# Three edits around the layer norms: how the deviation is found, who splits the first gate tile, and where three side products land

## The chip, the cores and the metric

The kernel runs on one core of a Trainium2 chip. A core has a matrix engine (TensorE, in rows PE, with its weight loads as PEld), a vector engine (VectorE, DVE), a scalar engine with function tables (ScalarE, ACT), GpSimd (POOL) and a sync engine that issues DMAs (SP). They run side by side and wait for each other by semaphores. The metric is the device time of one execution in microseconds. Times inside a profile are microseconds from the start of its span; unless said otherwise, they are of the first of the two layers.

## The reference

The input x has 512 tokens of width 2048. Two layers follow each other. Each makes y from x (the first by an attention of three branches and a gated recurrence, the second by a gated causal convolution of 31 taps with a layer norm of its own, then a product with an output matrix), and then both do the same, which is where the change lies:

```
mu  = mean(x);  var = mean((x - mu)**2)
layernorm(x) = (x - mu) * rsqrt(var + 1e-5) * g + b
x = layernorm(1.414 * x + y)                       # post norm of the layer
x = x + (p[i] @ ple_w[i]) * sigmoid(x @ ple_gate_w[i])
```

p[i] has 512 tokens of width 256, ple_w[i] is 256 x 2048 (the side product), ple_gate_w[i] is 2048 x 2048 (the gate). Everything is float32. There are three layer norms in all: the post norms of the two layers (numbers 0 and 2 in the code) and the one inside the convolution layer (number 1).

## The kernel before

Activations lie transposed: 16 chunks of 128 channels by 512 tokens, in SBUF buffers Y and Z. A weight matrix is a row of tiles of 128 x 2048 (all 16 input chunks for 128 output channels), 177 in all, counted by W_... constants. To keep float32 accuracy on fast matmuls, every operand is taken as a high and a low part: ACT rounds a tile into w_hi (`split` in the scalar block, line 769), then DVE (line 1117), or GpSimd in the convolution (line 363), forms w_lo as w_raw - w_hi. A gemm of one output chunk is 16 x 3 matmuls of 128 x 512: high by high, high by low, low by high (line 419 is the helper that issues all matmuls). SP loads the tiles into two slots; a tile's load waits until the tile that last had its slot is split, by the semaphore w_split, which counts splits in the order of the tiles. Gemms put their result into two PSUM banks G0 and G1 in turns; G_... constants count these uses, and bank_free0 and bank_free1 count how often each was emptied. Six more banks, X0 to X2 and T0 to T2, serve everything else. Each engine's order is written out by hand in its own block.

The stretch of the change is `second_part`, which stands in the blocks of PE, ACT and DVE and is run once per layer, with its counterpart `x1_low` on GpSimd:

1. The output projection: 16 gemms. DVE adds each result to the residual, subtracts a shift (the mean over the first channels), and adds up the values (ln_sum) and, from ACT's squares, the squares (ln_sqs). The last of these additions are lines 1456, 1462 and 1465; both inputs of each lie in SBUF.
2. The PLE pack: eight side products of this half of ple_w (c = 0 to 7), six matmuls each, which ACT copies from G0 or G1 into Z (`ple_out`, line 934). Between them PE does the norm's small work, in this order: products 0 and 1; `token_mean` and `token_var`, eight matmuls of one column each, that bring ln_sum into X0 and ln_sqs into T2, by token; products 2 and 3; `spread_mean` (two matmuls, a diagonal matrix by ones, into X1); product 4; `spread_dev` (the same for 1/deviation, into X2); products 5, 6 and 7.
3. `statistics` on DVE: mean, offset and variance as columns of four (lines 1477 to 1484), the mean's diagonal (line 1472), the split of the first gate tile, three small steps of Newton's method that refine ACT's guess of 1/deviation (lines 1491 to 1496), and its diagonal. The guess is made by `deviation` on ACT: logarithm, then exponential of minus half of it (lines 958 and 960). The two functions lie in different tables, each loaded ahead of it.
4. The chunks, j = 0 to 15: DVE subtracts the mean in X1 (line 1501, three ahead) and multiplies by 1/deviation in X2 (line 1505). ACT applies g and b (line 997), then rounds the chunk into a_hi (`x1_high`, line 773). GpSimd makes a_lo (line 340). ACT also empties side products 5 to 7 behind chunks 0, 1 and 2, and splits the second gate tile behind chunk 6; DVE forms its low part behind chunk 9.
5. The gate: `gemm_pair` runs the first two gate gemms interleaved, the second six chunks behind the first, and takes each chunk when its low part is there. Then 14 gemms follow. DVE combines, and GpSimd stores.

The layer norm of the convolution uses the same `statistics` and `deviation`; between its spread of the mean and that of the deviation PE does a whole gemm.

## Time and profile before

| | us |
|---|---|
| median of three timed runs | 2190.28 |
| the three runs | 2190.28, 2190.56, 2186.19 |
| the profiled execution | 2185.88 |
| its span (first to last instruction) | 2184.1 |
| mean granted TensorE clock, as a share of full | 0.994 |
| TensorE matmuls busy | 2148.8 (98%) |
| DVE busy | 1220.6 (56%) |
| ACT busy | 801.1 (37%) |
| GpSimd busy | 341.8 (16%) |

The busy shares are averages over very different stages. TensorE's matmuls overlap each other, so its 98% says that it seldom stands still, not that it runs at its peak. The profile also names, for each idle time, what ended it, and follows the chain of work that ended last back from the end: 95% of it are on PE.

### The profile page before, as it was taken

The page shows a single profiled execution, that of the slowest core. Times are in us where ns is not written, and L with a number is a line of the kernel's source. Part 1 is how long each engine was busy: PE and PEld are TensorE (multiplying, and loading weights), DVE is VectorE, ACT ScalarE, POOL GpSimd, SP SyncE. Part 2 cuts the span into 40 slices and gives each one's busy share as a digit, 9 for nine tenths or more (in the row PEclk, how much of TensorE's full clock was granted, in tenths as well). Part 3 has the DMA queues.
Part 4 walks back from the last instruction along what each step waited for, and adds up shares of the span by engine and source line. Part 5 has one row for each costly group of instructions (what it writes and reads, how often), then busy time and mean ns, then how long its engine had stood idle before and what let it go on. Part 6 is the DMA issues. An engine that isn't in the chain of part 4 may idle for free.

```text
span 2184.1 us, 27326 instructions
## 1 busy us (share of the span) xinstructions
PE 2148.8 (98%) x9916; PEld 1764.0 (81%) x9916; DVE 1220.6 (56%) x1986; ACT 801.1 (37%) x990; POOL 341.8 (16%) x179
## 2 busy tenths in 40 slices
PE   8999999999999999999899999999999999999998
PEld 7888878888888888788688778888888788886887
DVE  5224464554645646436733388888888764466332
ACT  3224364453544645312622232222323442126221
POOL 0000000000000000000300024444757430003000
PEclk9999999999999999999999999999999999999999
DMA  8222221122122212422233322222222234221331
GB/s 317 80 97 77 78 78 69 66 77 77 58 77 77 77 64 77 148 96 96 78 120 120 120 93 96 97 97 96 96 96 97 94 115 155 96 96 58 127 121 60
DMA packets 31551, 213.77 MB, mean 98 GB/s; under 512 B 3744, under 2 KB 3744, under 8 KB 7296
## 3 DMA queue, kind: packets, MB, share of 16 engines
q1 hardware_dynamic: 26928, 189.80, 24.3%
q0 software_dynamic: 4560, 23.20, 2.7%
q8 instruction: 31, 0.51, 0.1%
q14 instruction: 32, 0.26, 0.0%
HBM read 204.60 MB, written 8.39 MB: 98 GB/s over the span
## 4 chain that ended last, share of the span: by engine, by line
PE 95%; ACT 2%; DVE 1%; issue 1%; DMA 0%; POOL 0%; SPq 0%; DVEq 0%; ACTq 0%; POOLq 0%
PE G L419 86%; PE X L419 7%; PE T L419 1%; PE T L558 1%; ACT w_hi L769 1%; ACT Y L997 1%; DMA Z<-xT_in 0%; DVE w_lo L1117 0%; ACT a_hi L773 0%; DVE a_lo L1122 0%; POOL a_lo L340 0%; PE T L663 0%; DVE tmp L1472 0%; ACT Z L934 0%; DVE Y L1501 0%
## 5 line engine op out<-in xcount | busy, mean ns | idle before, releaser
L419 PE MATMUL G<-a_hi,w_hi 128*128 128x512 f32 (+1 forms) x2784 | 1092.4, 393 | 21.3 <-POOL a_lo L340 10.9
L419 PE MATMUL G<-a_lo,w_hi 128*128 128x512 f32 (+1 forms) x2784 | 1081.5, 389 | 0.0
L419 PE MATMUL G<-a_hi,w_lo 128*128 128x512 f32 x2752 | 1074.0, 390 | 0.0
L769 ACT ACTIVATE w_hi<-w_raw 128x2048 fp32r<-128x2048 f32 x175 | 335.1, 1915 | 1107.4 <-PE G L419 1103.1
L1117 DVE TENSOR_TENSOR w_lo<-w_raw,w_hi 128x2048 fp32r<-128x2048 f32 x128 | 293.5, 2293 | 691.8 <-ACT w_hi L769 691.8
L419 PEld LDWEIGHTS G<-a_hi,w_hi 128*128 128x128 f32 x2784 | 524.6, 188 | 138.9 <-POOL a_lo L340 16.2
L419 PEld LDWEIGHTS G<-a_lo,w_hi 128*128 128x128 f32 x2784 | 524.8, 189 | 107.7 <-issue 1.5
L419 PEld LDWEIGHTS G<-a_hi,w_lo 128*128 128x128 f32 x2752 | 518.2, 188 | 109.1
L1638 DVE SCALAR_TENSOR_TENSOR T<-tmp,par,T 128x512 f32<-128x512 f32 x464 | 306.9, 748 | 0.0
L363 POOL TENSOR_TENSOR w_lo<-w_raw,w_hi 128x2048 fp32r<-128x2048 f32 x46 | 212.5, 4619 | 247.8 <-ACT w_hi L769 247.8
L334 POOL DMA_DIRECT2D Y<-xT_in x4 | 2.1, 532 | 848.0 <-DVE a_lo L1122 848.0
L340 POOL TENSOR_TENSOR a_lo<-Y,a_hi 128x512 fp32r<-128x512 f32 x32 | 42.1, 1342 | 361.9 <-ACT a_hi L773 361.9
L419 PE MATMUL X<-Z 128*128 128x64 f32 (+7 forms) x544 | 96.5, 325 | 0.0
L419 PEld LDWEIGHTS X<-Z 128*128 128x128 f32 (+2 forms) x544 | 72.5, 181 | 22.9 <-issue 13.3
L1328 DVE COPY_PREDICATED tmp<-msk,X 128x256 f32<-128x256 uint8 (+2 forms) x48 | 23.4, 487 | 52.3 <-issue 34.8
L773 ACT ACTIVATE a_hi<-Y 128x512 fp32r<-128x512 f32 x80 | 47.0, 622 | 10.2 <-PE G L419 8.4
L1626 DVE TENSOR_TENSOR tmp<-G,tmp 128x512 f32<-128x512 f32 x16 | 11.0, 687 | 58.0 <-PE G L419 58.0
L952 ACT ACTIVATE tmp<-Y 128x512 f32 (+1 forms) x32 | 19.5, 630 | 63.9 <-DVE Y L1539 58.2
L847 ACT ACTIVATE Z<-Z,nmx 128x128 f32<-128x128 f32 (+1 forms) x64 | 35.2, 552 | 17.1 <-DVE nmx L1360 17.0
L1122 DVE TENSOR_TENSOR a_lo<-Y,a_hi 128x512 fp32r<-128x512 f32 x48 | 30.7, 686 | 14.5 <-ACT a_hi L773 14.4
L1501 DVE TENSOR_TENSOR Y<-Y,X 128x512 f32<-128x512 f32 x48 | 32.2, 678 | 11.6 <-PE X L419 11.6
L952 ACT ACTIVATE Z<-Y 128x512 f32 (+1 forms) x16 | 10.1, 633 | 77.6 <-POOL Y L380 72.8
(234 smaller groups left out, 1438.0 us busy)
## 6 DMA issues: line engine op xcount, KB each, us to landing
w_raw<-wall_in SPq DMA_DIRECT2D x175, 1024.0 KB, 4.8
Z<-xT_in SPq DMA_DIRECT2D x4, 1024.0 KB, 11.3
Y<-w_in POOLq DMA_DIRECT2D x2, 2048.0 KB, 18.9
Y<-xT_in POOLq DMA_DIRECT2D x4, 1024.0 KB, 5.0
x_residual<-Y POOLq DMA_DIRECT2D x16, 256.0 KB, 3.8
Y<-x_residual POOLq DMA_DIRECT2D x4, 1024.0 KB, 5.8
out<-Y POOLq DMA_DIRECT2D x16, 256.0 KB, 3.6
w_raw<-wall_in SPq DMA_DIRECT2D x8, 256.0 KB, 10.3
```

The lines of the kernel that those rows point to most:

```text
L340: pool.tensor_tensor(a_lo[:, j, :], chunk(Y, j), a_hi[:, j, :].bitcast(F), ALU.subtract).then_inc(S(f"x1_split{layer}"), 1)
L363: pool.tensor_tensor(w_lo[:, w.slot, :], w_raw[:, w.slot, :], w_hi[:, w.slot, :].bitcast(F), ALU.subtract).then_inc(S("w_split"), 1)
L419: return pe.matmul(o, l, r, start=start, stop=stop)
L769: f(w_hi[:, w.slot, :], w_raw[:, w.slot, :], ACT.Copy).then_inc(S("w_hi"), 1)
L773: f(a_hi[:, j, :], chunk(Y, j), ACT.Copy).then_inc(S(sem), 1)
L847: f(prob_of(ti), prob_of(ti), ACT.Exp, bias=nmx[:, o + ti:o + ti + 1], accum_out=rsum[:, o + ti:o + ti + 1]).then_inc(S("exps"), 1)
L952: f(dst, chunk(Y, c), ACT.Square).then_inc(S("squared"), 1)
L1117: tt(w_lo[:, w.slot, :], w_raw[:, w.slot, :], w_hi[:, w.slot, :].bitcast(F), ALU.subtract).then_inc(S("w_split"), 1)
L1122: tt(a_lo[:, j, :], src, a_hi[:, j, :].bitcast(F), ALU.subtract).then_inc(S(sem), 1)
L1328: dve.copy_predicated(dst[0:rows], m[0:rows], src[0:rows]).then_inc(S("level_copied"), 1)
L1501: tt(chunk(Y, j), chunk(Y, j), X[1][:, :], ALU.subtract).then_inc(S("less_mean"), 1)
L1638: stt(acc, src, cw, acc, op0=ALU.mult, op1=ALU.add).then_inc(S("tap"), 1)
```

## The change

`deviation` on ACT is now one square root. DVE takes its reciprocal as the guess, and no longer splits the first gate tile between the mean's diagonal and the Newton steps. A square root into a scratch column, `load_root_table`, stands earlier in ACT's order, so that the table is loaded there: ahead of the split of the first gate tile in `second_part`, and behind `silu_z(40, 8)` in the convolution. The first gate tile's low part is made by GpSimd, at the head of `x1_low`. Side products 5 to 7 of the second pack of each layer go into the banks T0, T1 and X0 and wait for none of them; the G counts shift by three per layer. ACT copies them behind the sixteenth chunk. DVE waits for the first gate tile's split before it splits the second, behind chunk 9.

```diff
--- before.py
+++ after.py
@@ -53,10 +53,11 @@
 W_CONV = 95
 W_TILES = 177
 
-G_PLE = ((61, 85), (157, 181))
-G_OUT = (69, 165)
-G_GATE = (93, 189)
-G_CONV = 109
+G_PLE = ((61, 85), (154, 178))
+G_OUT = (69, 162)
+G_GATE = (90, 183)
+G_CONV = 106
+LATE = 5
 LEVEL_ROWS = (64, 96, 128, 128, 128, 128)
 
 HALVES = (64, 32, 16, 8, 4, 2, 1)
@@ -109,7 +110,7 @@
 
 LN_COUNTS = dict(
     half_summed=4, shift_done=1, shift_ready=1, sums_set=3, centred=16, c_summed=16, squared=16, sq_summed=16, mean_sum=1,
-    var_sum=1, ln_step=6, var=1, ln_log=1, ln_guess=1, diag_d=1, diag_r=1, mean_spread=1, dev_spread=1, less_mean=16, normed=16)
+    var_sum=1, ln_step=6, var=1, ln_root=1, ln_guess=1, diag_d=1, diag_r=1, mean_spread=1, dev_spread=1, less_mean=16, normed=16)
 
 
 class Idx:
@@ -184,6 +185,7 @@
         rsum = sb("rsum", [P, 12])
         rg = sb("rg", [P, 12])
         eglast = sb("eglast", [P, NT])
+        act_scratch = sb("act_scratch", [P, 1])[:, :]
         stat = sb("stat", [P, 5 * NT])
         lb = sb("lb", [P, 4, HEADS])
         ident = par[:, C_ID:C_ID + P]
@@ -259,6 +261,7 @@
         X = [pb("X0"), pb("X1"), pb("X2")]
         TB = [pb("T0"), pb("T1"), pb("T2")]
         O = X[0]
+        LATE_BANKS = (TB[0], TB[1], X[0])
         NEAR_BANKS = (X[1], TB[2])
         LEVEL_AT = (None, (X[2], 0), (X[2], 256), (X[0], 0), (X[0], 256), (X[1], 0), (X[1], 256))
         LEVEL_BANK_DONE = (1, 3, 3, 5, 5, 7, 7)
@@ -335,6 +338,11 @@
 
             def x1_low(layer):
 
+                w = Idx(W_GATE[layer])
+                pool.wait_ge(S("w_hi"), w.n(1))
+                pool.wait_ge(S("w_split"), w.n())
+                pool.tensor_tensor(w_lo[:, w.slot, :], w_raw[:, w.slot, :], w_hi[:, w.slot, :].bitcast(F),
+                                   ALU.subtract).then_inc(S("w_split"), 1)
                 for j in range(KC):
                     pool.wait_ge(S(f"x1_hi{layer}"), j + 1)
                     pool.tensor_tensor(a_lo[:, j, :], chunk(Y, j), a_hi[:, j, :].bitcast(F), ALU.subtract).then_inc(
@@ -479,9 +487,12 @@
                     if c == 0:
                         pe.wait_ge(S("w_split"), w.n(1))
                         pe.wait_ge(S("p_split"), layer + 1)
-                    g = Idx(G_PLE[layer][u] + c)
-                    pe.wait_ge(S(f"bank_free{g.slot}"), g.half())
-                    o = G[g.slot][:, :]
+                    if u == 1 and c >= LATE:
+                        o = LATE_BANKS[c - LATE][:, :]
+                    else:
+                        g = Idx(G_PLE[layer][u] + c)
+                        pe.wait_ge(S(f"bank_free{g.slot}"), g.half())
+                        o = G[g.slot][:, :]
                     for k in range(PLE_K):
                         at = (c * PLE_K + k) * P
                         hi, lo = w_hi[:, w.slot, at:at + P], w_lo[:, w.slot, at:at + P]
@@ -931,7 +942,10 @@
                     act.wait_ge(S("gemm_done"), W_PLE[layer][u] + 1)
                 else:
                     act.wait_ge(S("ple_done"), 14 * layer + 7 * u + c + 1)
-                frees(f(chunk(Z, 8 * u + c), G[g.slot][:, :], ACT.Copy), g)
+                if u == 1 and c >= LATE:
+                    f(chunk(Z, 8 * u + c), LATE_BANKS[c - LATE][:, :], ACT.Copy)
+                else:
+                    frees(f(chunk(Z, 8 * u + c), G[g.slot][:, :], ACT.Copy), g)
 
 
             prev_hz(HEADS, Idx(W_PLE[0][0] - 1))
@@ -955,9 +969,10 @@
 
                 var, dev = stat[:, 2 * NT:3 * NT], stat[:, 3 * NT:4 * NT]
                 act.wait_ge(*after("var", n, 1))
-                f(dev, var, ACT.Ln).then_inc(S("ln_log"), 1)
-                act.wait_ge(*after("ln_log", n, 1))
-                f(dev, dev, ACT.Exp, scale=-0.5).then_inc(S("ln_guess"), 1)
+                f(dev, var, ACT.Sqrt).then_inc(S("ln_root"), 1)
+
+            def load_root_table():
+                f(act_scratch, ones[:, 0:1], ACT.Sqrt)
 
             def second_part(layer):
                 w, g = W_OUT[layer], G_OUT[layer]
@@ -980,6 +995,7 @@
                             c = 3 + 2 * k + n
                             square(n_ln, i * 4 + c, ln_sq[c % 2], i * 4 + (c - 1))
 
+                load_root_table()
                 split(Idx(w + 17))
                 square(n_ln, KC - 1, ln_sq[1], KC - 2)
                 ple_out(layer, 1, 0)
@@ -1000,10 +1016,11 @@
                         x1_high(j - 1)
                     elif j < 3:
                         x1_high(j)
-                        ple_out(layer, 1, j + 5)
                     if j == 6:
                         split(Idx(w + 18))
                 x1_high(KC - 1)
+                for c in range(LATE, 8):
+                    ple_out(layer, 1, c)
 
                 def gate(w, g, n_out):
                     act.wait_ge(S("gemm_done"), w.n(1))
@@ -1078,6 +1095,7 @@
 
             split(Idx(W_CONV + 42))
             silu_z(40, 8)
+            load_root_table()
             square(1, KC - 2, c_sq[0], KC - 2)
             square(1, KC - 1, c_sq[1], None)
             deviation(1)
@@ -1464,7 +1482,7 @@
                 dve.wait_ge(*after("sq_summed", n, c))
                 tt(sqs, sqs, sq, ALU.add).then_inc(S("sq_summed"), 1)
 
-            def statistics(n, diag_of_mean, between=None):
+            def statistics(n, diag_of_mean):
 
                 mean, off, var, dev, rr = [stat[:, k * NT:(k + 1) * NT] for k in range(5)]
 
@@ -1484,9 +1502,8 @@
                 stt(var, TB[2][:, 0:NT], 1.0 / D, off, op0=ALU.mult, op1=ALU.add).then_inc(S("var"), 1)
                 dve.wait_ge(*after("centred", n, KC))
                 spread(diag_of_mean, mean).then_inc(S("diag_d"), 1)
-                if between:
-                    between()
-
+                dve.wait_ge(*after("ln_root", n, 1))
+                dve.reciprocal(dev, dev).then_inc(S("ln_guess"), 1)
                 dve.wait_ge(*after("ln_guess", n, 1))
                 stt(rr, dev, -0.5, dev, op0=ALU.mult, op1=ALU.mult).then_inc(step, 1)
                 dve.wait_ge(*after("ln_step", n, 4))
@@ -1568,7 +1585,7 @@
                 dve.wait_ge(*drained(Idx(g + 15)))
                 centre(n_ln, KC - 1)
                 add_last(n_ln, KC - 1, ln_sqs, ln_sq[1])
-                statistics(n_ln, diag_d, lambda: split(Idx(w + 17)))
+                statistics(n_ln, diag_d)
                 dve.wait_ge(*after("mean_spread", n_ln, 1))
                 for j in range(3):
                     minus_mean(j)
@@ -1578,6 +1595,7 @@
                     if j + 3 < KC:
                         minus_mean(j + 3)
                     if j == 9:
+                        dve.wait_ge(S("w_split"), w + 18)
                         split(Idx(w + 18))
 
                 def gate(g, j, n_gate):
```

## Rows read from the trace of the kernel before

**Rows 1.** The page, part 1: engine, busy us (share of the span), instructions.
```profile
PE 2148.8 (98%) x9916; PEld 1764.0 (81%) x9916; DVE 1220.6 (56%) x1986; ACT 801.1 (37%) x990; POOL 341.8 (16%) x179
```
**Rows 2.** The view of waits, TensorE: in total, times, longest.
```profile
PE G L419 <- POOL a_lo L340: 10.9, 10, 2.9
```
**Rows 3.** The chain that ended last: start us, us, engine, tile and line.
```profile
1067.95 0.49 ACT Z L934
...
1076.53 1.81 ACT w_hi L769
...
1079.63 2.17 POOL a_lo L340
...
1733.02 0.86 PE X L419 x2
```
**Rows 4.** Timeline of ACT: start, us, engine, line, operation [idle before, releaser].
```profile
1055.37 1.92 ACT L769 ACTIVATE w_hi<-w_raw 128x2048 fp32r<-128x2048 f32 x1 [3.90 <-PE G L419]
1057.20 0.61 ACT L952 ACTIVATE tmp<-Y 128x512 f32<-128x512 f32 x1
...
1058.79 1.28 ACT L958 ACT_TABLE_LOAD   x1
1060.09 0.20 ACT L958 ACTIVATE stat<-stat 128x4 f32<-128x4 f32 x1
...
1096.50 1.92 ACT L769 ACTIVATE w_hi<-w_raw 128x2048 fp32r<-128x2048 f32 x1 [6.61 <-PE G L419]
```
**Rows 5.** Timeline of DVE, in the same columns.
```profile
1056.76 0.69 DVE L1462 TENSOR_TENSOR tmp<-tmp,Y 128x512 f32<-128x512 f32 x1
1057.84 0.69 DVE L1465 TENSOR_TENSOR tmp<-tmp 128x512 f32<-128x512 f32 x1 [0.39 <-ACT tmp L952]
...
1059.83 0.16 DVE L1484 SCALAR_TENSOR_TENSOR stat<-T,stat 128x4 f32<-128x4 f32 x1 [0.40 <-PE T L419]
...
1063.90 1.87 DVE L1501 TENSOR_TENSOR Y<-Y,X 128x512 f32<-128x512 f32 x3
1065.75 0.69 DVE L1505 TENSOR_TENSOR Y<-Y,X 128x512 f32<-128x512 f32 x1
...
1077.11 0.68 DVE L1501 TENSOR_TENSOR Y<-Y,X 128x512 f32<-128x512 f32 x1
1078.36 2.29 DVE L1117 TENSOR_TENSOR w_lo<-w_raw,w_hi 128x2048 fp32r<-128x2048 f32 x1 [0.57 <-ACT w_hi L769]
...
1733.91 0.69 DVE L1501 TENSOR_TENSOR Y<-Y,X 128x512 f32<-128x512 f32 x1 [11.55 <-PE X L419]
```
**Rows 6.** Timeline of TensorE: the variance matmuls and the two spreads.
```profile
1058.69 1.03 PE L419 MATMUL T<-ones,tmp 128*128 128x1 f32 x8
...
1062.44 1.02 PE L419 MATMUL X<-tmp,ones 128*128 128x512 f32 x2
...
1064.68 1.02 PE L419 MATMUL X<-tmp,ones 128*128 128x512 f32 x2
```
**Rows 7.** Lines 1456 and 340 (min/median/max ns), and timelines of DVE and GpSimd.
```profile
L1456 DVE TENSOR_TENSOR Y<-Y,tmp x4: 678/692/3907, 1056.0 to 1977.9; 128x512 f32<-128x512 f32 x4
...
L340 POOL TENSOR_TENSOR a_lo<-Y,a_hi x32: 1276/1289/2158, 1068.0 to 2013.6; 128x512 fp32r<-128x512 f32 x32
...
1779.53 4.60 POOL L363 TENSOR_TENSOR w_lo<-w_raw,w_hi 128x2048 fp32r<-128x2048 f32 x1 [6.25 <-ACT w_hi L769]
1780.04 4.64 DVE L1663 TENSOR_TENSOR Y<-Y,Z 128x512 f32<-128x512 f32 x1 [5.61 <-ACT Z L1051]
```
**Rows 8.** Timeline of TensorE behind the convolution norm and at the second layer's gate.
```profile
1719.35 1.91 PE L419 MATMUL X<-tmp,ones 128*128 128x512 f32 x2 [0.93 <-DVE tmp L1472]
...
1723.10 0.40 PE L419 MATMUL G<-a_hi,w_lo 128*128 128x512 f32 x1
...
2003.72 0.80 PE L419 MATMUL G<-a_hi,w_hi 128*128 128x512 f32 x1 [2.22 <-POOL a_lo L340]
...
2010.02 0.40 PE L419 MATMUL G<-a_hi,w_hi 128*128 128x512 f32 x1
```

## The prediction

> **What bounds the kernel now.** I read the page first. TensorE is busy for 98% of the span [rows 1], so an edit pays only where TensorE waits. The view of waits names the largest wait: its matmuls wait for GpSimd's low parts, 10.9 us in ten places [rows 2]. The chain of waits puts them: after the output projection of each of the two layers, where the post norm runs. Among its links there are ACT's side-product copies, its weight split, and one GpSimd row of 2.17 us, behind which the gate matmuls go on at 1081.84 [rows 3]. Then I read this stretch engine by engine [rows 4, 5, 6]. The second layer repeats it 921.9 us later with the same distances to a few hundredths, so I work out the first and double it.
>
> The profiled execution took 2185.88 us, of which 1.78 lie outside its span of 2184.1. The median of the three timed runs is 2190.28; one of them is at 2186.19. The sum is made on the profiled one.
>
> **Root and reciprocal.** Two table loads go (each as the one from 1058.79 to 1060.09, 1.30 us [rows 4]), and so does a DVE split inside the statistics, of 2.29 us like that of 1078.36 [rows 5]. One load comes ahead of the weight split at 1055.37; ACT is idle for 3.90 us before that [rows 4], so it is hidden. But what do the norms wait for? The deviations are spread by a TensorE pair at 1064.68, which stands in program order behind side products 2 to 4 and the mean's pair at 1062.44 [rows 6]. Without loads and split the diagonal is done about 1062.0: variance at 1059.83 + 0.16 = 1059.99, root and reciprocal about 0.2 each like the four-column rows, three steps of 0.2, one of 0.7. So 2.7 us of slack hide it. What a root and a reciprocal of four columns take, no row here shows: between nothing and the 0.69 of a 512-column DVE row, both inside the slack. What is late next is TensorE itself. The mean's pair lands at 1062.44 + 0.89 = 1063.33, where DVE began at 1063.90 [rows 5]; the deviations' pair at 1064.68 + 0.89 = 1065.57, where DVE began at 1065.75. (0.89 is what lies between such a pair's start at 1733.02 and its reader's at 1733.91 [rows 3, 5].) Gain: 0.18 us per layer. In the convolution's norm nothing waits for the deviations until a whole gemm later: 0.
>
> By the Trainium skill, page "ScalarE: Activation LUTs", section "What ACT_TABLE_LOAD costs", each switch takes about 2.66 us with its drain; the rows have 1.30 from the load's start to the activation's. By the page two loads would be worth 5.3 us on ACT, by the rows 2.6; in the sum both are 0.18.
>
> **Three side products in free banks.** TensorE no longer waits for a bank at the last product and at the gate's start, some tenths; but it then waits for low parts, so that is worth 0. ACT has three copies fewer between the first chunks: 0.49 each on the chain [rows 3], 1.47 in all. GpSimd's seventh low part, asked for at 1079.63, is asked for at 1079.63 - 1.47 - 0.18 = 1077.98. It does not start then. Before, it took 2.17 us, as against a usual 1.29 [rows 7], because DVE's split of 1078.36 held it until 1080.65; it ended 1.14 behind that. Now the split starts at DVE's next slot, 1077.11 + 0.60 - 0.18 = 1077.53 (its high part is there at 1076.53 + 1.81 - 1.65 = 1076.69), ends at 1079.82, and the low part at 1080.96. The gate matmuls go on at 1081.01: gain 0.83 us per layer instead of 1.65, the 0.18 included. The three copies come back behind the last chunk, where ACT idles for 6.61 us ahead of 1096.50 [rows 4]; without that cover they would cost 1.5.
>
> **The gate's first low part on GpSimd.** Its high part is there at 1055.37 + 1.92 = 1057.29. GpSimd has no other work then: the residual's four DMA issues ahead of it in its queue were done before the first out chunk, and the low parts behind it wait for normed chunks, the first of which DVE begins at 1065.75. So it starts at about 1057.37, and takes 4.6 us. SP's next weight load waits for this split; even at 1062.1 it is issued earlier than before, and it is for ACT's row of 1096.50: 0.
>
> What runs beside it on DVE? The sum of squares, with two inputs in SBUF, at 1057.84 [rows 5]; TensorE's variance matmuls wait for it and start at 1058.69 [rows 6]. The trace shows such pairs. A DVE add of two SBUF tiles takes 0.69, and 3.91 where a GpSimd split is under way [rows 7]; one that came 0.51 us behind GpSimd's start (1780.04 behind 1779.53) took 4.64 and ended 0.55 behind GpSimd's end. DVE rows that read PSUM keep their 0.68. Here GpSimd is 0.47 ahead; DVE's sum of 1056.76 may hold it until 1057.45. Then GpSimd ends at 1062.05, the sum of squares at 1062.60 instead of 1058.53, and the variance matmuls start at 1062.65 instead of 1058.69: 3.96 us lost, with TensorE idle and all that follows in program order shifted whole (side products 2 to 7, both spreads, the norm, the low parts). The 2.7 us of slack above do not help, since variance and side products shift together. Bounds: below, 0 (no hold; nothing in it makes TensorE earlier than 1058.69, where the mean's matmuls end); above, the whole 4.6.
>
> The Trainium skill, page "SBUF — State Buffer", section "Who interferes with whom", says that a VectorE instruction with two SBUF inputs and a GpSimd one that reads SBUF exclude each other for the whole instruction, the first one winning. The rows agree (3.91 and 4.64 for 0.69). It goes further than they do: an instruction of four columns would be held too, which in the first rival below would make the loss 1.9 us per layer instead of 1.4.
>
> **The clock.** TensorE's idle 4 us stand between 16 one-column matmuls [rows 6]. In the convolution's norm 16 such matmuls and 0.93 us of idle are followed by a fall to the low level: from 1719.35 to the sixth gate matmul at 1723.10 are 3.75 us, where full clock (0.45 + 0.64 + 4 x 0.23) makes 2.01 [rows 8]: price 1.7. At the gate of the second layer 15 intervals from 2003.72 to 2010.02 take 6.30, where full clock (0.34 + 14 x 0.23) makes 3.56: price 2.7 [rows 8]. So a fall behind the new stall costs 0 to 2.7 per layer; I take 1.7, the nearest row. The fall at the gate itself stays; the idle before it is 3.9 us instead of 2.9, and its price I leave; since the two falls shown differ by 1.0, it may move by that.
>
> **Sum.** Per layer 3.96 - 0.83 + 1.7 = 4.8; two layers 9.7 us slower. On the profiled execution 2195.5, on the median 2200.0. Since the timed runs lie at both levels, I take 2198. This case's own range: 2 x 3.13 = 6.3 without falls to 2 x (3.13 + 2.7) = 11.7, that is 2192 to 2202.
>
> **Rivals.**
> 1. DVE first (0.12). If DVE's sum of squares gets in before GpSimd, GpSimd holds from 1058.53 to 1063.15, and the mean's diagonal, DVE's next 512-column row with two SBUF inputs, due at 1059.9, ends at 1063.15 + 0.65 = 1063.8, for a pair due at 1062.44: 1.4 lost, 0.8 won, 1.1 us slower in all: 2187 to 2191.4. For it: only 0.47 us separate the two. Against it: 0.51 was enough for GpSimd, and a start like its others (0.08 behind the high part) is 0.39 ahead at the least.
> 2. No hold at this place (0.10): the sum of squares keeps 0.69, since GpSimd takes the read side only after its start, more than 0.47 later. The change then wins 0.83 per layer: 1.7 faster, 2188.6; if the later low part isn't held either, it ends at 1079.3, and 2.5 per layer make 2185.3. It decides at once: any hold over 0.83 us turns it to slower. Against it: the pairs shown were held for the rest of the other engine's instruction.
> 3. The clock falls far longer than any row shows (0.06): over 2204.
> 4. The root's table isn't the one in force when it comes, and a load of 1.3 stands before it: hidden by the 2.7 us, the same time as the forecast, so no chance of its own.
>
> **How the numbers follow.** The forecast has 0.72. Range 2191 to 2203: it takes in the forecast's bounds, the upper end of rival 1, and leaves out rival 2 and the long fall. A change under 0.2% (4.4 us) can't be told from none here. Slower by more than that: the forecast but for a rest (0.70) and rival 3: 0.76. Within it: rival 1, the smaller form of rival 2, and the rest: 0.19. Faster: 0.05.
>
> **What would show it.** The sum of squares (line 1465 before) at about 4.7 us instead of 0.69 in both layers, with a GpSimd split of 4.6 from 1057.4; TensorE's variance matmuls at 1062.6 behind a wait of 4 us for DVE; a granted clock under 1 in the stretch behind. The norms then stand 3.8 us later throughout, the split of the next tile on DVE beside a GpSimd low part of 3.0 us, and the gate goes on near 1085 (1086.7 with the fall). No table load between the variance and the gates. The prediction is wrong if the sum of squares keeps 0.69, or if DVE gets in first.

## The result, and the profile after

| | before | after |
|---|---|---|
| median of five runs, us | 2187.50 | 2199.52 |
| lowest to highest | 2186.19 to 2190.56 | 2199.23 to 2201.00 |
| profiled execution | 2185.88 | 2199.23 |
| its span | 2184.1 | 2197.2 |
| mean granted TensorE clock | 0.994 | 0.992 |

The ratio is 1.0053, with an interval of 1.0038 to 1.0067: the change costs 12 us. 2198 was forecast, in a range of 2191 to 2203. The ratios, here and below, are estimates with a 95% interval and can differ in the fourth place from the quotient of the two medians. Two executions far outside all others, one of before with 9306.75 us and one of f_again with 7727.82, fell in a slow state and are left out of the medians.

The page after, part 1, in the columns of [rows 1]:

```profile
PE 2152.5 (98%) x9916; PEld 1768.2 (80%) x9916; DVE 1224.5 (56%) x1987; ACT 797.6 (36%) x987; POOL 352.3 (16%) x181
```

The busy shares hardly move, since 13 us are 0.6% of the span. The view of waits does say where they are; it is of TensorE, and answers to [rows 2]:

```profile
PE G L427 <- POOL a_lo L348: 11.7, 12, 3.7
...
PE T L427 <- DVE tmp L1483: 7.3, 2, 3.7
```

The first line is the old wait for low parts, 0.8 longer. The second is new: T is the bank of the variance, and its matmuls wait twice, 3.7 us each, for DVE's sum of squares. GpSimd and DVE in this stretch, in the columns of [rows 5], first layer:

```profile
1058.77 4.51 POOL L344 TENSOR_TENSOR w_lo<-w_raw,w_hi 128x2048 fp32r<-128x2048 f32 x1 [165.19 <-ACT w_hi L780]
...
1086.06 10.45 POOL L348 TENSOR_TENSOR a_lo<-Y,a_hi 128x512 fp32r<-128x512 f32 x7 [1.70 <-ACT a_hi L784]
```

```profile
1059.23 4.59 DVE L1483 TENSOR_TENSOR tmp<-tmp 128x512 f32<-128x512 f32 x1 [0.39 <-ACT tmp L966]
...
1066.54 0.17 DVE L1506 RECIPROCAL stat<-stat 128x4 f32<-128x4 f32 x1
...
1071.38 1.88 DVE L1518 TENSOR_TENSOR Y<-Y,X 128x512 f32<-128x512 f32 x3 [3.36 <-PE X L427]
1073.62 0.69 DVE L1522 TENSOR_TENSOR Y<-Y,X 128x512 f32<-128x512 f32 x1 [0.36 <-PE X L427]
...
1085.58 2.28 DVE L1135 TENSOR_TENSOR w_lo<-w_raw,w_hi 128x2048 fp32r<-128x2048 f32 x1
```

The sum of squares comes 0.46 us behind GpSimd's split and takes 4.59 instead of 0.69 [rows 5]. TensorE waits for it and then runs slower, as the timeline of TensorE shows:

```profile
1059.27 0.95 PE L427 MATMUL X<-ones,tmp 128*128 128x1 f32 x8
1063.88 1.87 PE L427 MATMUL T<-ones,tmp 128*128 128x1 f32 x8 [3.66 <-DVE tmp L1483]
...
1066.61 0.63 PE L427 MATMUL G<-p_hi,w_lo 128*128 128x512 f32 x1
...
1070.31 1.02 PE L427 MATMUL X<-tmp,ones 128*128 128x512 f32 x2
...
1072.56 1.02 PE L427 MATMUL X<-tmp,ones 128*128 128x512 f32 x2
...
1089.05 0.50 PE L427 MATMUL G<-a_hi,w_hi 128*128 128x512 f32 x1 [3.67 <-POOL a_lo L348]
```

The view by windows (stretch; length; busy us and instructions of PE, PEld, DVE, ACT, POOL; granted clock; DMA share; GB/s) has the granted clock at 0.50 for the five us that begin 0.88 before the end of the stall, which is the lower of its two levels (1.2 and 2.4 GHz), and at 0.84 for the next five:

```profile
1063.00:1068.00 5.00, 4.12 (x14) 3.64 (x15) 3.23 (x11) 0.21 (x1) 0.28 (x1) 0.50 0.59 210
1068.00:1073.00 5.00, 5.00 (x18) 3.50 (x17) 1.64 (x4) 1.43 (x3) 0.00 (x0) 0.84 0.00 0
```

ACT's table load is where the diff put it, under an idle time. Behind the variance there is one root and no load:

```profile
1052.88 1.28 ACT L975 ACT_TABLE_LOAD   x1
1056.77 1.92 ACT L780 ACTIVATE w_hi<-w_raw 128x2048 fp32r<-128x2048 f32 x1 [2.39 <-PE G L427]
...
1066.05 0.21 ACT L972 ACTIVATE stat<-stat 128x4 f32<-128x4 f32 x1 [5.88 <-DVE stat L1502]
```

Runs of different kernels are best laid over each other at the start of the mean's matmuls, which comes before the first thing that the change can delay. The table has, from there, where TensorE starts the variance's matmuls, the two spreads, the gate's seventh chunk (at which it takes up again after its wait), and the last matmul of the gate's pair. f_again is f_behind_diag once more, on another chip. Distances in us, read from each kernel's timeline of TensorE, first layer; in brackets the second layer.

| kernel | variance | mean's spread | deviations' spread | 7th chunk | end of pair |
|---|---|---|---|---|---|
| before | 0.81 | 4.56 | 6.80 | 23.96 (23.96) | 42.89 (44.36) |
| after | 4.61 | 11.04 | 13.29 | 29.78 (29.25) | 49.00 (48.42) |
| a_pool_only | 4.61 | 10.65 | 12.90 | 30.13 (30.20) | 49.23 (49.40) |
| b_no_pool | 0.82 | 4.56 | 6.81 | 23.47 (23.46) | 42.64 (43.87) |
| c_root_only | 0.81 | 4.56 | 6.80 | 24.10 (24.10) | 43.29 (43.08) |
| d_late_only | 0.81 | 4.56 | 6.81 | 23.30 (23.31) | 42.50 (42.22) |
| e_behind_squares | 0.82 | 6.39 | 8.74 | 25.23 (25.23) | 45.18 (44.46) |
| f_behind_diag | 0.81 | 4.56 | 6.81 | 23.30 (23.30) | 42.51 (42.50) |
| f_again | 0.81 | 4.56 | 6.80 | 23.30 (23.31) | 42.26 (42.45) |
| g_quarters | 1.37 | 6.71 | 8.96 | 25.45 (25.46) | 45.28 (44.64) |
| h_psum_square | 0.81 | 5.14 | 7.50 | 23.99 (23.99) | 44.43 (44.43) |
| i_second_split_at_8 | 0.81 | 4.56 | 6.80 | 22.58 (22.59) | 41.76 (41.80) |
| j_both_splits_early | 0.81 | 4.56 | 6.80 | 23.13 (23.12) | 40.98 (41.03) |
| k_lag_5 | 0.81 | 4.56 | 6.81 | 23.12 (23.11) | 40.74 (42.11) |

After the change the seventh chunk is 5.82 and 5.29 us later, the pair's end 6.11 and 4.06: 10.2 of the profiled span's 13.1. Of the rest, 1.4 had come before the mean's matmuls of the first layer (1059.27 against 1057.88), from clock falls at the start-up; 1.6 lie behind the first layer, where after a wait of 2.16 for a weight split the clock fell at 1270.79 and before it did not. No edit touches either place.

### The profile page after: what moved, and what is told of

Read it like the earlier page. It is cut to its first block, busy times and chain, and to the rows that moved or that the text cites. A ratio compares the mean times of both kernels' runs of the same rounds, so it can differ in the third digit from the quotient of the medians.

```text
span 2197.2 us, 27322 instructions
## 1 busy us (share of the span) xinstructions
PE 2152.5 (98%) x9916; PEld 1768.2 (80%) x9916; DVE 1224.5 (56%) x1987; ACT 797.6 (36%) x987; POOL 352.3 (16%) x181
## 4 chain that ended last, share of the span: by engine, by line
PE 95%; ACT 2%; DVE 1%; issue 1%; DMA 0%; POOL 0%; SPq 0%; DVEq 0%; ACTq 0%; POOLq 0%
PE G L427 86%; PE X L427 7%; PE T L427 1%; PE T L569 1%; ACT w_hi L780 1%; ACT Y L1013 1%; DMA Z<-xT_in 0%; DVE tmp L1483 0%; ACT a_hi L784 0%; DVE w_lo L1135 0%; DVE a_lo L1140 0%; POOL a_lo L348 0%; PE T L674 0%; PE T L679 0%; PE T L546 0%
## 5 line engine op out<-in xcount | busy, mean ns | idle before, releaser
L1135 DVE TENSOR_TENSOR w_lo<-w_raw,w_hi 128x2048 fp32r<-128x2048 f32 x126 | 288.9, 2293 | 692.4 <-ACT w_hi L780 692.4
L371 POOL TENSOR_TENSOR w_lo<-w_raw,w_hi 128x2048 fp32r<-128x2048 f32 x46 | 212.4, 4618 | 249.6 <-ACT w_hi L780 249.6
L344 POOL TENSOR_TENSOR w_lo<-w_raw,w_hi 128x2048 fp32r<-128x2048 f32 x2 | 9.0, 4508 | 332.6 <-ACT w_hi L780 332.6
L784 ACT ACTIVATE a_hi<-Y 128x512 fp32r<-128x512 f32 x80 | 46.8, 621 | 10.2 <-PE G L427 8.4
## 6 DMA issues: line engine op xcount, KB each, us to landing
Z<-xT_in SPq DMA_DIRECT2D x4, 1024.0 KB, 11.5
```

The source lines that it names most:

```text
L371: pool.tensor_tensor(w_lo[:, w.slot, :], w_raw[:, w.slot, :], w_hi[:, w.slot, :].bitcast(F), ALU.subtract).then_inc(S("w_split"), 1)
L784: f(a_hi[:, j, :], chunk(Y, j), ACT.Copy).then_inc(S(sem), 1)
L1135: tt(w_lo[:, w.slot, :], w_raw[:, w.slot, :], w_hi[:, w.slot, :].bitcast(F), ALU.subtract).then_inc(S("w_split"), 1)
```

## The experiments

The theory: the whole loss is GpSimd's split holding DVE's sum of squares, together with the clock that falls behind the stall. The rivals: the root and the late copies have a share in it; or the split costs at any place.

**a_pool_only, b_no_pool, c_root_only, d_late_only** take the change apart. From before, a_pool_only has only the split moved:

```diff
+                pool.tensor_tensor(w_lo[:, w.slot, :], w_raw[:, w.slot, :], w_hi[:, w.slot, :].bitcast(F),
+                                   ALU.subtract).then_inc(S("w_split"), 1)
...
-                statistics(n_ln, diag_d, lambda: split(Idx(w + 17)))
+                statistics(n_ln, diag_d)
```

DVE also waits for the first gate tile's split ahead of that of the second, as in the whole change. b_no_pool is the whole change with these lines turned round, c_root_only has the root and the reciprocal alone (DVE's split stays between the mean's diagonal and the reciprocal), d_late_only the three late side products alone.

> The kernel before with one edit of the three: the first gate tile's low part by GpSimd. Theory 1 (GpSimd's split holds DVE's sum of squares, and TensorE stands behind it): the whole loss is here. The sum of squares takes 4.6 us in both layers, TensorE's variance matmuls wait 3.7 us for it, the clock falls behind it. Per layer 3.8 for the hold and 1.7 to 2.7 for the fall, nothing back: 11 to 13 us slower than before, more than the full change by the 1.3 us that the side products give back. Theory 2 (the loss comes of the late side products or of the table load ahead of the weight split, and the held sum would be hidden): within 3 us of before.

> The full change without this one edit: DVE splits the first gate tile inside the statistics, as before. Theory 1: the sum of squares is back at 0.69 us, no wait of TensorE ahead of the variance matmuls, no fall of the clock there, and the late side products bring the seventh low part 0.66 us earlier per layer: 1 to 2 us faster than before (2185 to 2187 where before has 2187.5). Theory 2: still 8 us or more slower than before.

> The kernel before with one edit: root and reciprocal in place of logarithm and exponential, the table loaded ahead. The spread of the deviations is bound by TensorE's order (side products 2 to 4 ahead of it), not by ACT or DVE. Theory 1: no change, within 0.5 us in the trace from the norm to the gate. Rival: the two table loads of 1.3 us were on the way to the norm, and 2.6 us per layer come back: 5 us faster.

> The kernel before with one edit: side products 5 to 7 in T0, T1 and X0, copied behind the chunks. Theory 1 (GpSimd's seventh low part is held by DVE's split of the second gate tile): the seventh chunk's high part comes 1.47 us earlier, the low part ends only 0.6 to 0.7 earlier and takes 2.9 us instead of 2.17; gain 0.65 per layer, 1.3 us in all. Rival (the low part simply follows its chunk): it takes 1.3 us, the gate goes on 1.5 us or more earlier, 3 us faster in all.

| kernel | runs | median us | ratio to before | interval |
|---|---|---|---|---|
| a_pool_only | 5 | 2198.25 | 1.0050 | 1.0036 to 1.0064 |
| b_no_pool | 11 | 2185.40 | 0.9992 | 0.9983 to 1.0001 |
| c_root_only | 11 | 2188.53 | 1.0004 | 0.9995 to 1.0013 |
| d_late_only | 11 | 2185.01 | 0.9986 | 0.9977 to 0.9995 |

The median of before on that chip was 2186.74. The split alone costs 11.5, where the whole change costs 12, and without it nothing is lost. It had been expected to cost 1.3 more than the whole change, which has the late side products' gain. The traces bear that out, with a seventh chunk 0.35 and 0.95 later than after's in the two layers; the medians, from two chips, do not, and their intervals are too wide to tell. Its rows on DVE and TensorE are those of after:

```profile
1059.36 4.60 DVE L1470 TENSOR_TENSOR tmp<-tmp 128x512 f32<-128x512 f32 x1 [0.39 <-ACT tmp L957]
```

```profile
1064.01 1.87 PE L424 MATMUL T<-ones,tmp 128*128 128x1 f32 x8 [3.66 <-DVE tmp L1470]
```

d_late_only brings the seventh chunk forward by 0.66 per layer. c_root_only brings nothing: in the table its spreads stand where they stood, and the seventh chunk is 0.14 later. DVE's timeline has the reason:

```profile
1062.73 2.28 DVE L1121 TENSOR_TENSOR w_lo<-w_raw,w_hi 128x2048 fp32r<-128x2048 f32 x1
1064.93 0.17 DVE L1494 RECIPROCAL stat<-stat 128x4 f32<-128x4 f32 x1
...
1066.33 1.88 DVE L1506 TENSOR_TENSOR Y<-Y,X 128x512 f32<-128x512 f32 x3
1068.13 0.68 DVE L1510 TENSOR_TENSOR Y<-Y,X 128x512 f32<-128x512 f32 x1
```

With the split still on DVE, its rows from the mean's diagonal to the norm follow each other without idle time, and the reciprocal's 0.20 adds to them. Counted from the mean's matmuls (1060.10), the subtractions begin at 6.23 instead of 6.02 and the first product with 1/deviation at 8.03 instead of 7.87. b_no_pool has both rows too, and its seventh chunk is 0.17 behind d_late_only's. With the split on GpSimd and out of the way DVE waits for the spreads, and the reciprocal costs nothing: f_behind_diag, below, has 23.30 like d_late_only.

**e_behind_squares, f_behind_diag**: where does the split cost nothing? Both are the whole change, with GpSimd made to wait ahead of its split, for the last sum of squares or for the deviations' diagonal:

```diff
+                pool.wait_ge(*after("sq_summed", 2 * layer, KC))    # e_behind_squares
+                pool.wait_ge(*after("diag_r", 2 * layer, 1))        # f_behind_diag
                 pool.wait_ge(S("w_hi"), w.n(1))
```

> The full change, but GpSimd's split of the first gate tile waits until DVE's sum of squares is done, and so comes between that and the mean's diagonal. Theory 1, form A (every DVE instruction with two SBUF inputs is held, four columns too): the sum of squares keeps 0.69, and the offset step (four columns, both inputs the mean) waits for the end of GpSimd's 4.5 us; the mean's diagonal comes 1.9 us late for TensorE; 1.9 - 0.66 per layer, 2.5 us slower than before in all, more if the clock falls. Form B (only the wide instructions are held): the offset step takes 0.16, the diagonal of 512 columns waits: 1.2 to 1.3 late, 1.2 us slower in all. Theory 2 (no hold by GpSimd): no wait at all, 1.3 us faster than before.

> The full change, but GpSimd's split waits until DVE has made the deviations' diagonal. From there on DVE's instructions read PSUM on one side. Theory 1: no DVE instruction is held; the split lies beside the subtractions of the mean and is over before the first low part; TensorE's stalls are those of the kernel with DVE's split in its old place: 1 to 2 us faster than before. Rival (a GpSimd split beside these subtractions slows them too, or comes too late for the gate): subtractions over 0.7 us, or a wait of the first gate matmul, and no gain.

The median of before on this chip was 2186.56, for these two and the next two. e_behind_squares: 2191.30 (7 runs), ratio 1.0022 (1.0011 to 1.0034). f_behind_diag: 2184.91 (11 runs), ratio 0.9994 (0.9985 to 1.0003). The timeline of DVE in e_behind_squares:

```profile
1057.61 0.69 DVE L1484 TENSOR_TENSOR tmp<-tmp 128x512 f32<-128x512 f32 x1 [0.39 <-ACT tmp L967]
1058.64 0.16 DVE L1496 TENSOR_SCALAR stat<-X 128x4 f32<-128x4 f32 x1 [0.34 <-PE X L428]
1058.84 4.14 DVE L1498 SCALAR_TENSOR_TENSOR stat<-stat 128x4 f32<-128x4 f32 x1
```

and its split on GpSimd:

```profile
1058.39 4.58 POOL L345 TENSOR_TENSOR w_lo<-w_raw,w_hi 128x2048 fp32r<-128x2048 f32 x1 [166.44 <-DVE tmp L1484]
```

The sum of squares is free again at 0.69. The mean's columns, read from a PSUM bank, keep 0.16 inside the split. The next row is four columns wide, has both inputs in SBUF, and takes 4.14, to 1062.98, where the split ends at 1062.97. So an instruction of four columns is held like one of 512, which [rows 7] did not show. The seventh chunk is 1.27 later per layer than before, which makes the 2.5 expected; the pair's end is 2.3 later in the first layer and 0.1 in the second, and the median 4.7. What makes up the difference is not shown; I take it for the spread of clock falls, and can't put it to one row. There is no fall behind this stall itself, though TensorE waits 1.66 us for the mean's diagonal:

```profile
1064.04 1.13 PE L428 MATMUL X<-tmp,ones 128*128 128x512 f32 x2 [1.66 <-DVE tmp L1491]
...
1065.23 0.40 PE L428 MATMUL G<-p_lo,w_hi 128*128 128x512 f32 x1
```

The matmuls behind it keep 0.40, and the granted clock from 1064 to 1069 is 1.00.

In f_behind_diag the split stands beside rows that read the spreads in PSUM. Both engines keep their times:

```profile
1061.81 4.58 POOL L345 TENSOR_TENSOR w_lo<-w_raw,w_hi 128x2048 fp32r<-128x2048 f32 x1 [169.92 <-DVE tmp L1491]
...
1077.92 5.43 POOL L349 TENSOR_TENSOR a_lo<-Y,a_hi 128x512 fp32r<-128x512 f32 x3 [1.70 <-ACT a_hi L785]
```

```profile
1063.23 1.88 DVE L1519 TENSOR_TENSOR Y<-Y,X 128x512 f32<-128x512 f32 x3 [1.50 <-PE X L428]
1065.48 0.69 DVE L1523 TENSOR_TENSOR Y<-Y,X 128x512 f32<-128x512 f32 x1 [0.37 <-PE X L428]
...
1077.44 2.28 DVE L1136 TENSOR_TENSOR w_lo<-w_raw,w_hi 128x2048 fp32r<-128x2048 f32 x1
```

The last row is the bound that is left: DVE's split of the second gate tile at 1077.44 stands 0.48 ahead of GpSimd's seventh low part, the first of the three at 1077.92, which takes 2.94, not 1.29. TensorE goes on when it has ended, at 1080.91.

**g_quarters, h_psum_square**: what exactly is held? g_quarters makes GpSimd's split four instructions of 512 columns. h_psum_square takes away one of the two SBUF inputs of the sum of squares, by having ACT square the last chunk into bank T0:

```diff
+                for q in range(4):                                   # g_quarters
+                    last = pool.tensor_tensor(w_lo[:, w.slot, quarter(q)], w_raw[:, w.slot, quarter(q)], ...
...
-                square(n_ln, KC - 1, ln_sq[1], KC - 2)               # h_psum_square
+                square(n_ln, KC - 1, TB[0][:, :], None)
...
-                add_last(n_ln, KC - 1, ln_sqs, ln_sq[1])
+                add_last(n_ln, KC - 1, ln_sqs, TB[0][:, :])
```

> The full change, with GpSimd's split cut into four instructions of 512 columns each, in the same place and with nothing that makes it wait. Theory 1 (the hold lasts for one instruction, the other engine gets in between): the sum of squares waits for one quarter only, 0.7 to 1.9 us long instead of 4.6; some more waits of up to 1.2 us each in the statistics; TensorE loses 0.7 to 2 us per layer, gains 0.66, and the clock does not fall ahead of the spreads: 0 to 3 us slower than before. Rival (GpSimd keeps the port from one instruction to the next): as the full change, 4.6 us or more, 11 us slower.

> The full change, but ACT writes the last chunk's squares into bank T0, so that DVE's last sum of squares has one input in SBUF and one in PSUM; GpSimd's split starts as in the full change. Theory 1: with one SBUF input the sum is not held, 0.69 us, and TensorE's variance matmuls start at once; the first instruction with two SBUF inputs behind it waits for GpSimd's end. Form A: that is the offset step, and the mean's diagonal is 0.8 us late; form B: the diagonal, 0.2 late. Less the 0.66 of the side products: within 1 us of before. Rival (DVE is held by any GpSimd instruction, whatever its inputs): as the full change.

g_quarters: 2191.84 (10 runs), ratio 1.0023 (1.0014 to 1.0032). h_psum_square: 2187.61 (10 runs), ratio 1.0003 (0.9993 to 1.0012). DVE in g_quarters, where the four pieces on GpSimd take 5.41 from 1057.31:

```profile
1057.78 1.36 DVE L1485 TENSOR_TENSOR tmp<-tmp 128x512 f32<-128x512 f32 x1 [0.39 <-ACT tmp L968]
...
1059.24 1.04 DVE L1499 SCALAR_TENSOR_TENSOR stat<-stat 128x4 f32<-128x4 f32 x1
1060.31 1.22 DVE L1501 TENSOR_SCALAR stat<-stat 128x4 f32<-128x4 f32 x1
1061.64 1.63 DVE L1492 TENSOR_TENSOR tmp<-par,stat 128x512 f32<-128x512 f32 x1
```

A hold lasts for one instruction: a DVE row gets in at each gap between pieces, and pays up to one piece. Four rows pay once each. The seventh chunk is 1.49 later per layer, 2.98 in all and inside the 0 to 3 expected; the median is 5.3 above before's, which is outside. The expectation that the clock would not fall ahead of the spreads failed too:

```profile
1059.19 1.05 PE L429 MATMUL T<-ones,tmp 128*128 128x1 f32 x8 [0.42 <-DVE tmp L1485]
...
1060.97 0.63 PE L429 MATMUL G<-p_hi,w_hi 128*128 128x512 f32 x1
...
1064.53 1.02 PE L429 MATMUL X<-tmp,ones 128*128 128x512 f32 x2
```

TensorE idles 0.42 between the one-column matmuls. Behind that the side products' matmuls take 0.63 instead of 0.39, with a granted clock of 0.50 from 1061 to 1064. The variance is 0.56 late and the mean's spread 2.15, so this fall costs 1.59, and as much in the second layer.

The third of the held rows has a single input in SBUF, which I had not expected to be held. The Trainium skill, page "SBUF — State Buffer", section "Who interferes with whom", says that VectorE's tensor_scalar can take the shared port pair with a single input too, in its two-port modes; this row, with 1.22 for 0.17, agrees that it is held; in which mode it ran no row shows.

DVE in h_psum_square:

```profile
1059.45 0.69 DVE L1483 TENSOR_TENSOR tmp<-tmp,T 128x512 f32<-128x512 f32 x1 [0.36 <-ACT T L966]
...
1060.71 2.91 DVE L1497 SCALAR_TENSOR_TENSOR stat<-stat 128x4 f32<-128x4 f32 x1
```

GpSimd's split runs from 1059.02 to 1063.60. The same sum, with one input in PSUM, keeps 0.69 in the middle of it. The hold moves to the next row with two inputs in SBUF, four columns wide, from 1060.71 to 1063.62. TensorE has side products 2 and 3 meanwhile, so only 0.58 of it reaches the mean's spread. The median is 1.05 above before's, where within 1 us had been expected, and its interval takes in no difference.

**f_again, i_second_split_at_8, j_both_splits_early** ask whether the next wait can be bought off. From f_behind_diag, the second gate tile's split moves on DVE ahead of GpSimd's seventh low part (i), or both its halves move far ahead (j):

```diff
-                    if j == 6:        # ACT, in j_both_splits_early
+                    if j == 2:
                         split(Idx(w + 18))
...
-                    if j == 9:        # DVE; j == 8 in i_second_split_at_8
+                    if j == 4:
                         dve.wait_ge(S("w_split"), w + 18)
```

> GpSimd's split behind the deviations' diagonal, once more, as the base of the next three on the same chip: 1 to 2 us faster than before, the seventh low part 2.9 us long, held by DVE's split of the second gate tile.

> As the base, with DVE's split of the second gate tile behind chunk 8 instead of 9. Its high part is there at about 1076.6 (in the base's times), where the split began at 1077.44, so it begins and ends 0.7 to 0.8 earlier. Theory 1: the seventh low part ends with it, 2.1 us long instead of 2.9, and the gate goes on 0.8 us earlier per layer, 1.5 us in all. Rival (the low part's length is its own, and follows its high part): 2.9 us still, no gain.

> As the base, with ACT's split of the second gate tile behind chunk 2 instead of 6, and DVE's behind chunk 4 instead of 9. DVE's split then lies where GpSimd waits for ACT anyway: GpSimd's fourth low part is held for 0.2 us, and the seventh ends near 1079.3 instead of 1080.9 at its usual 1.3 us. The gate's seventh chunk begins 1.5 us earlier; TensorE's longest single wait there falls from 3.7 to about 2 us, a new one ahead of the fourth chunk is 3 us. Theory 1: 1.5 us per layer faster than the base, 4 us faster than before. Rival (the wait only moves, since ACT's and DVE's work for the chunks is as long): as the base.

| kernel | runs | median us | ratio to before | interval |
|---|---|---|---|---|
| f_again | 11 | 2185.16 | 0.9995 | 0.9986 to 1.0004 |
| i_second_split_at_8 | 11 | 2184.96 | 0.9987 | 0.9978 to 0.9995 |
| j_both_splits_early | 11 | 2183.64 | 0.9983 | 0.9975 to 0.9992 |

The median of before here was 2186.84. i's seventh chunk is 0.72 earlier than f's, as the longest low part falls from 2.94 to 2.23. That is as expected. Its pair ends 0.50 and 0.65 earlier than f_again's; its median of 0.2 less says nothing at this noise. In j DVE splits at 1074.00, and GpSimd's longest low part is down to 1.52. The rows are those of DVE, of GpSimd, and of TensorE at the fourth and fifth chunk:

```profile
1074.00 2.29 DVE L1136 TENSOR_TENSOR w_lo<-w_raw,w_hi 128x2048 fp32r<-128x2048 f32 x1 [0.79 <-ACT w_hi L781]
```

```profile
1075.90 1.52 POOL L349 TENSOR_TENSOR a_lo<-Y,a_hi 128x512 fp32r<-128x512 f32 x1 [2.44 <-ACT a_hi L785]
1078.34 8.79 POOL L349 TENSOR_TENSOR a_lo<-Y,a_hi 128x512 fp32r<-128x512 f32 x7 [0.92 <-ACT a_hi L785]
```

```profile
1077.47 0.80 PE L428 MATMUL G<-a_hi,w_hi 128*128 128x512 f32 x1 [2.99 <-POOL a_lo L349]
1079.67 0.80 PE L428 MATMUL G<-a_hi,w_hi 128*128 128x512 f32 x1 [0.55 <-POOL a_lo L349]
```

The wait is still there, 2.99 where f has 3.66, but it comes at an earlier chunk, and the pair ends 1.5 us sooner than f_behind_diag's in each layer, 1.3 and 1.4 sooner than f_again's. How it comes about is not as expected. The seventh chunk should have begun 1.5 earlier and begins 0.17 earlier, so there the rival, that the wait only moves, is nearly right. The rest is won behind it: from the seventh chunk to the pair's end j takes 17.85 and f_behind_diag 19.21. In j the matmuls of low clock stand from 1077.47, the fourth chunk, to 1082.83, when TensorE still has a wait in between; in f_behind_diag they stand from 1081.48 to 1084.46, behind the last wait. j is the fastest kernel of the study, 3.2 us ahead of before with its interval wholly below 1. What bounds this stretch there is the arrival of the low parts, in the view of waits:

```profile
PE G L428 <- POOL a_lo L349: 8.3, 8, 3.0
```

**k_lag_5** is j with the second gemm of the pair five chunks behind the first instead of six:

```diff
-                gemm_pair(w, g, f"x1_split{layer}")
+                gemm_pair(w, g, f"x1_split{layer}", LAG=5)
```

> As the one with both splits early, and the second gate gemm five chunks behind the first instead of six. TensorE finds work 1.25 us earlier behind the fifth chunk (0.6 won, as it runs half idle there), but between the first gemm's end and the second's there is 0.7 us less for ACT's and DVE's splits of the third tile (1.92 + 2.29 against 4.1 with six chunks): the third gemm waits 0.7 us. Theory: equal to it within 0.5 us.

2185.59 (11 runs), ratio 0.9993 (0.9984 to 1.0002): 2 us above j. The third gate gemm now waits 0.39 for its weight split,

```profile
1099.40 0.49 PE L428 MATMUL G<-a_hi,w_hi 128*128 128x512 f32 x1 [0.39 <-DVE w_lo L1136]
```

and while the pair of the first layer ends 0.24 earlier than j's, that of the second ends 1.1 later. The reason lies in where the clock falls. Behind the wait for the fourth chunk j's matmuls are slow at once, in both layers; k's of the second layer are not, and turn slow at the fifth chunk:

```profile
1998.13 0.50 PE L428 MATMUL G<-a_hi,w_hi 128*128 128x512 f32 x1 [2.98 <-POOL a_lo L349]
...
2000.32 0.79 PE L428 MATMUL G<-a_hi,w_hi 128*128 128x512 f32 x1 [1.23 <-POOL a_lo L349]
...
2006.38 0.39 PE L428 MATMUL G<-a_hi,w_lo 128*128 128x512 f32 x1
```

From the fifth chunk's first matmul to the fourteenth behind it, that is from the second row to the third, are 6.06 us in k and 4.99 in j: this is the 1.1. The view by windows shows the same, k_lag_5 first and then j_both_splits_early:

```profile
2005.00:2010.00 5.00, 5.00 (x20) 4.06 (x20) 3.31 (x6) 5.00 (x10) 5.00 (x5) 0.87 0.00 0
```

```profile
2005.00:2010.00 5.00, 5.00 (x23) 4.12 (x22) 4.18 (x7) 5.00 (x9) 5.00 (x5) 1.00 0.00 0
```

k has 20 matmuls in these five us and j 23, though the stretch lies 0.87 later behind the mean's matmuls in k. The low clock lasts about as long in both, 6.1 us from 2000.32 to 2006.38 in k and 5.8 from 1999.01 to 2004.77 in j; but in k it comes later, on matmuls with no wait between them. The expectation of no difference was a miss. Why the clock fell one chunk later in this execution is open, and so is whether it does so in others.

## Why the prediction was right, step by step

**The hold (right in kind, 0.16 too large).** Forecast: GpSimd's 4.6 holds the sum of squares, the variance's matmuls 3.96 late. Measured: 3.80 in the first layer (4.61 - 0.81). The split took 4.51, not 4.60, and DVE ended 0.54 behind it, as in [rows 7]. GpSimd was 0.46 ahead of DVE, where 0.47 had been worked out. Half of the 0.16 is the split's length, and the other half the 0.08 for which the prediction had let DVE's earlier sum hold GpSimd, which it did not. Rival 1 never came up, and rival 2, no hold, fell with the 4.59. That this edit alone makes the loss is shown by a_pool_only and b_no_pool; that it does so by the hold, by f_behind_diag, where the same split holds nothing and costs nothing. That a DVE row with one of its two inputs in PSUM escapes is shown by h_psum_square.

**The clock (right that it falls, the size too small).** Forecast 1.7 per layer, from the nearest row, between 0 and 2.7 [rows 8]. Measured: the mean's spread should come at 4.56 + 3.80 = 8.36 and comes at 11.04 and 10.51: 2.68 and 2.15, inside the bounds and near their upper end. In a_pool_only it was 2.29 and 2.39. What was mis-sized is this term. The row it was taken from has an idle time of 0.93, the stall here one of 3.66. g_quarters has a stall of 0.42 at the very same place, and its fall costs 1.6. So the price rises with the idle time, but far less than in proportion: nine times the stall makes 1.3 to 1.7 times the price. The prediction's claim that a fall follows at all fits the place: behind the stalls of e_behind_squares (1.66) and h_psum_square (0.42), which follow twelve matmuls of 512 columns and not eight of one column, the granted clock stays at 1.00.

**The late copies (right).** Forecast 0.83 with the root's 0.18 included, so 0.65 by themselves. d_late_only measured 0.66 per layer, and its low part is held for the same reason and as long as worked out: 2.94 at the most, where 1080.96 - 1077.98 made 2.98.

**The root and reciprocal (wrong by 0.18 per layer).** The loads' cover held: no row of TensorE moves in c_root_only up to the second spread. The gain of 0.18 did not come. It rested on 0.89 us from a spread's start to DVE's row, taken from the convolution. In this stretch it is 1.06, 1072.56 to 1073.62 after; before it was 1.07, 1064.68 [rows 6] to 1065.75 [rows 5]. DVE's row of 1065.75 stood 0.05 behind its own slot (1063.90 and three rows at 0.60 each), and so waited for the matmuls already: a sooner diagonal had nothing to give. The price of the root, 0.21, and of the reciprocal, 0.17, lie where the estimate had them.

**The sum.** At the seventh chunk of the first layer: 3.80 + 2.68 - 0.66 = 5.82, which is the table's difference to the hundredth; of the second 3.80 + 2.15 - 0.66 = 5.29. (The clock's term is itself read from this kernel's spreads; what the sum tests is that the 0.66 of d_late_only comes back behind them.) Forecast 4.8. At the pair's end the gate's own fall, left open in the forecast, takes or gives some: 6.11 and 4.06. Two layers make 10.2 (forecast 9.7), and the medians differ by 12.0; the other 1.8 are not placed, and in the two profiles the corresponding rest is clock falls elsewhere. The forecast time of 2198 is nearer to 2199.52 than its working deserves: the median that it started from, 2190.28, was of three runs, and five gave 2187.50. As a difference the change was forecast 2.3 us too cheap.

## What to carry to other kernels

Before work moves to an idle GpSimd, look at which DVE rows run beside it: in these runs every one with two inputs in SBUF, even of four columns, waited for the end of the GpSimd instruction that had come first, and a lead of half a microsecond decided over four. Put such work beside DVE rows that read PSUM; here the same split costs 11.5 us at one place and nothing 3 us later. Then look at what TensorE does around a stall. Between one-column matmuls it counted twice, once for its length and once for the clock behind it, even at 0.42 us; behind a dozen wide matmuls it counted once.

## What the runs showed of the hardware that I had not expected

- A DVE row of 128 x 4 elements with both inputs in SBUF took 4.14 and 2.91 us beside a GpSimd split, for 0.16. The section of the Trainium skill that the prediction cites ("SBUF — State Buffer", "Who interferes with whom") makes no exception for short instructions, and these rows agree; the rows of before did not show it.
- A DVE tensor_scalar with a single input in SBUF was held too, 1.22 us for 0.17 beside pieces of GpSimd, and 1.21 in the second layer.
- A stall of 3.7 us between one-column matmuls drew a clock fall in both layers of after and in a_pool_only, at a price of 2.15 to 2.68 us; one of 0.42 at the same place, in g_quarters, drew one of 1.6. Stalls of 1.66 and 0.42 behind twelve side-product matmuls drew none.
- One and the same kernel, before, ran between 2184.4 and 2190.6 over 35 runs on one chip. Where I compared two profiles, differences of 1.4 and 1.6 us were clock falls at places that the change doesn't touch. With 10 to 12 runs against about 30 of before, the intervals above are still 0.0009 to either side, or 2 us: a smaller difference than that is not settled here by the medians.
